# Sixteen gate units as seven half-size products each, beside a running recurrence

## The reference, cut to what matters

```
h     = rmsnorm(x)
proj  = h @ w_in                       # q, k, v | r, k, v of the recurrence | gates (4096 columns)
o_a   = diff_attention(q, k, v)        # 8 heads
o_b   = rwkv7(proj)                    # 32 heads of 64; 4 chunks of 64 tokens; state S per head
gates = sigmoid(proj[gate columns] + b_gate)
mix   = (gates[:2048] * (o_a @ w_branch_a) + gates[2048:] * (o_b @ w_branch_b)) @ w_out
x     = x + rmsnorm(mix);  x = x + rmsnorm(swiglu(rmsnorm(x)));  then the second block
```

## Time and profile before

| | us |
|---|---|
| median of 3 runs (3976.82 to 3977.19) | 3977.06 |
| the profiled execution | 3979.2 |
| its span | 3977.4 |
| TensorE busy | 3846.1 (97%) |
| VectorE busy | 1747.7 (44%) |
| GpSimd busy | 1233.2 (31%) |
| ScalarE busy | 599.5 (15%) |

### The profile page before, as it was taken

The page is one execution under the profiler, slowest core; times in us unless marked ns, Lnnn a source line. Parts: engine busy times, 40 slices in busy tenths (PEclk is TensorE's granted clock), DMA queues, the critical chain, the costliest instruction groups (busy, mean ns, idle before and its releaser), DMA issues.

```text
span 3977.4 us, 65016 instructions
## 1 busy us (share of the span) xinstructions
PE 3846.1 (97%) x28196; PEld 3553.6 (89%) x28196; DVE 1747.7 (44%) x3073; ACT 599.5 (15%) x1314; POOL 1233.2 (31%) x779
## 2 busy tenths in 40 slices
PE   8999999999999998999999999989998899999997
PEld 7888888888878998999999998878797899999997
DVE  1344425550121623111125446552522688888544
ACT  0333311111111111000000000132402211111001
POOL 0000000003320865777760000000250577775000
PEclk9999999999999998999999999999999999999999
DMA  6566654457553443444445454428242344444542
GB/s 229 211 221 219 219 214 159 176 187 225 181 193 139 175 149 117 168 167 168 169 162 170 162 188 183 156 103 227 81 159 85 124 167 168 167 167 159 175 157 78
DMA packets 109117, 668.80 MB, mean 168 GB/s; under 512 B 23056, under 2 KB 27472, under 8 KB 78496
## 3 DMA queue, kind: packets, MB, share of 16 engines
q1 hardware_dynamic: 64208, 549.01, 38.2%
q0 software_dynamic: 21088, 69.73, 6.0%
q10 hardware_dynamic: 23536, 45.92, 3.2%
HBM read 611.34 MB, written 53.25 MB: 167 GB/s over the span
## 4 chain that ended last, share of the span: by engine, by line
PE 92%; DVE 3%; ACT 2%; issue 1%; POOL 1%; POOLq 1%; DVEq 1%; DMA 0%; ACTq 0%
PE product_bank L553 47%; PE product_bank L601 31%; PE product_bank L395 3%; PE mixer_bank L745 1%; PE mixer_bank L761 1%; ACT xT L862 0%; PE mixer_bank L1274 0%; PE mixer_bank L1288 0%; PE mixer_bank L1125 0%; POOL arena L525 0%; POOLq L524 0%; POOL arena L522 0%; POOLq L521 0%; PE product_bank L2237 0%; PE mixer_bank L2199 0%
## 5 line engine op out<-in xcount | busy, mean ns | idle before, releaser
L601 PE MATMUL product_bank<-hT,weight_ring 128*128 128x256 f32 x3712 | 825.0, 380 | 1.6 <-ACT out_stage L640 1.6
L601 PEld LDWEIGHTS product_bank<-hT,weight_ring 128*128 128x128 f32 x3712 | 700.6, 190 | 106.2 <-issue 12.0
L553 PE MATMUL product_bank<-hT,weight_ring 128*128 128x128 f32 x3648 | 453.6, 276 | 11.0 <-DVEq L1631 5.8
L553 PEld LDWEIGHTS product_bank<-hT,weight_ring 128*128 128x128 f32 x3648 | 432.2, 193 | 13.1 <-DVEq L1631 6.0
L553 PE MATMUL product_bank<-arena,weight_ring 128*128 128x128 f32 x3168 | 394.6, 275 | 0.0
L553 PEld LDWEIGHTS product_bank<-arena,weight_ring 128*128 128x128 f32 x3168 | 374.8, 192 | 0.6
L577 DVE TENSOR_TENSOR arena<-product_bank,arena 128x128 f32<-128x128 f32 x126 | 36.7, 291 | 721.1 <-PE product_bank L553 721.1
L520 POOL TENSOR_TENSOR arena<-weight_ring 128x1024 f32<-128x1024 f32 x88 | 211.0, 2398 | 449.7 <-PE product_bank L553 279.6
L2626 DVE SCALAR_TENSOR_TENSOR arena<-arena 128x256 f32<-128x256 f32 x176 | 321.8, 1867 | 14.6 <-ACT arena L2591 11.2
L523 POOL TENSOR_TENSOR weight_ring<-weight_ring 128x1024 f32<-128x1024 f32 x110 | 270.0, 2455 | 0.0
L553 PE MATMUL product_bank<-hT,arena 128*128 128x128 f32 x2016 | 247.4, 277 | 0.1
(11 more groups left out here) (494 smaller groups left out, 5303.5 us busy)
## 6 DMA issues: line engine op xcount, KB each, us to landing
weight_ring<-in_weights SPq DMA_DIRECT2D x213, 2048.0 KB, 8.0
weight_ring<-in_weights SPq DMA_DIRECT2D x128, 512.0 KB, 5.7
weight_ring<-in_weights SPq DMA_DIRECT2D x64, 384.0 KB, 5.7
units<-out_stage ACTq DMA_DIRECT2D x87, 256.0 KB, 7.8
rwkv_keep<-arena ACTq DMA_DIRECT2D x16, 1282.0 KB, 6.3
arena<-rwkv_keep POOLq DMA_DIRECT2D x8, 1280.0 KB, 7.2
arena<-units POOLq DMA_DIRECT2D x36, 256.0 KB, 3.4
arena<-units POOLq DMA_DIRECT2D x48, 128.0 KB, 6.0
```

The source lines that it names most:

```text
L553: mm = pe.matmul(bank[:, at * P:at * P + P], lhs[:, j, :], rhs[:, j, :], start=g == 0 and n in (0, 3) and j == 0, stop=g == n_groups - 1 a ...
L601: mm = pe.matmul(psg[b][:, half * T:half * T + T], lhs, rhs, start=k == 0, stop=k == 15)
```

## The change

Part 1: the gate units are done as sevens, in two groups of four block pairs each, so that a unit is 14 products of 8 records. A unit still has four pieces in TensorE's list, now of 4, 3, 4 and 3 products. The four combinations of the source are made at the start of the kernel into `xT`, which is loaded again from its input during the `out` stage, as are two constants whose space is used.

Part 2: GpSimd makes the weight sums of a group into one buffer per group, so the sum for (unit u, group g) waits until TensorE has used (u - 1, g). The sums of unit 0 stand in the list of the heads, behind the wait for head 5; the others in `rw2_pool`, with the operands' transfers between them.

Part 3: VectorE's list gets the gates' recombinations: the one of unit u stands at quarter 186 + 4u. ScalarE stores the unit's result a unit later.

Part 4: a half's operands come in 8 and 7 transfers instead of 20 and 19; the first group's second half, its last transfer and the storing of the inverse go to SyncE's queue.

```diff
@@ stream_weights
+                if n == UNIT_AT["gates", 6][0]:
+                    store_inverse(sp)
+                if n == UNIT_AT["gates", 8][0]:
+                    rw2_operands(sp, 0, 1)
+                    rw2_rest(sp, 0)
+                if n == UNIT_AT["out", 0][0]:
+                    load_again(sp)
@@
-        SEVENS = ("branch_b", "out", "ffn_in", "ffn_out", "out2", "up2", "down2")
+        SEVENS = ("gates", "branch_b", "out", "ffn_in", "ffn_out", "out2", "up2", "down2")
+        EARLY = ("gates",)
+        GROUPS_OF = {n: GROUPS if n in LONG else 2 if n in EARLY else 1 for n in SEVENS}
@@
+        def early_quarters(pe, name, src, combined, sums):
+            half = lambda blocks, g: [v[:, 4 * g:4 * g + 4, :] for v in blocks]
+            for u in range(PLAN[name].units):
+                steps = unit_sevens(pe, name, u, lambda g: half(source_blocks(src), g), lambda g: sums(u, g),
+                                    lambda g: half(combined, g))
+                for n, _ in enumerate(steps):
+                    if n in (3, 6, 10):
+                        yield
+                yield
@@
+        def rw2_operands(eng, n, half):
+            if n == 0:
+                eng.wait_ge(sem("inverse_stored"), 16)
+                eng.wait_ge(sem("attn_head_done"), DA_HEADS)
+            else:
+                eng.wait_ge(sem("rw2_Y_sum"), NCH * (n - 1) + 2 * half + 2)
...
+            for par in range(2):
+                for head in range(2):
+                    eng.dma_start(r2m[tokens(head, par), :, 2 * head + half, :],
+                                  mu[GT * n:GT * n + GT, par, half, :, head, :].rearrange("g s t -> s g t")).then_inc(got, 16)
@@ rw2_pool
-                    for g in range(GT):
-                        for par in range(2):
-                            for head in range(2):
-                                pool.dma_start(r2m[tokens(head, par), g, 2 * head + half, :],
-                                               mu[GT * n + g, par, half, :, head, :]).then_inc(got, 16)
...
+            for u, g in [(u, g) for u in range(1, 6) for g in range(2)] + [(6, 0)]:
+                sum_gates(pool, u, g)
+            rw2_operands(pool, 0, 0)
+            between = {(9, 1): (1, 0), (11, 0): (1, 1), (12, 0): (1, None), (13, 1): (2, 0), (15, 0): (2, 1), (15, 1): (2, None)}
+            for u, g in [(6, 1)] + [(u, g) for u in range(7, 16) for g in range(2)]:
+                sum_gates(pool, u, g)
+                if (u, g) in between:
+                    n, half = between[u, g]
+                    if half is None:
+                        rw2_rest(pool, n)
+                    else:
+                        rw2_operands(pool, n, half)
@@ da_pool
                 if h >= 2:
                     pool.wait_ge(sem("attn_head_done"), h - 1)
...
+                if h == 7:
+                    sum_gates(pool, 0, 0)
+                    sum_gates(pool, 0, 1)
@@
+        def sum_gates(pool, u, g):
+            if u:
+                group_used(pool, "gates", u - 1, g)
+            sum_weights(pool, "gates", u, g, gates_sums_of(u, g))
@@
+        def gates_product_dve(dve):
+            yield
+            for u in range(16):
+                for _ in range(4):
+                    yield
+                row, o = gates_kept(u)
+                wait(dve, stored[o], 16 * (row // RING))
+                kept_ = ostage[:, o, :]
+                recombine_dve(dve, "gates", u, gates_first[u % 2], *gates_temps, kept_[:, 0:T], kept_[:, T:2 * T])
+                dve.drain().then_inc(sem("gates_kept"), 1)
@@ VectorE's list
-            run(rw1_dve(dve))
-            weave(inv_dve(dve), da_dve(dve), inverse_steps)
-            run(rw2_dve(dve))
+            combine_source_dve(dve, "gates", source_blocks(hT), early_combined)
...
+            elsewhere = (None for _ in range(4 * 45))
+            dense = chain(elsewhere, gates_product_dve(dve))
+            beside(dense, rw1_dve(dve), beside_rw1, RW1_LEAD)
+            beside(dense, heads_and_inverse(), beside_da, DA_LEAD)
+            beside(dense, rw2_dve(dve), beside_rw2, RW2_LEAD)
```

More of the change, by code:

```diff
@@ L452, in group_used @@
         def group_used(eng, name, u, g):
-            pos, half = group_pos(name, u, g)
-            if name in LONG and half == 0:
+            pos = group_pos(name, u, g)[0]
+            if GROUPS_OF.get(name, 1) > 1 and g % 2 == 0:
                 eng.wait_ge(sem("sevens_halves_used"), sevens_half(name, u, g))
@@ L1229, in rw2_pe, with rw2_rest_loaded @@
+        def rw2_loads(half, n):
+            if half and n == 0:
+                return "rw2_first_in1", 16 * 7
+            return f"rw2_in{half}", 16 * (8 - half) * (n + 1 - half)
+        def rw2_rest_loaded(n):
+            return ("rw2_in_all", 16 * n) if n else ("rw2_first_in_all", 16)
         def rw2_pe(pe):
@@ L1373, in group @@
                         last = dve.tensor_tensor(obT[:, b, :], d, kept_all("g", g), ALU.mult)
-                last.then_inc(sem("rw2_group_done"), 1)
-                yield
+                    if pair == GT // 2 - 1:
+                        last.then_inc(sem("rw2_group_done"), 1)
+                    yield
             for n in range(RW_TILES // GT):
@@ L1555, in build, with gates_sums_of, gates_kept, store_gates @@
         bb_out = [arena[:, at:at + 512].rearrange("p (h t) -> p h t", h=2) for at in (12288, 13836)]
+        early_combined = combined_source(xT)
+        flat_y = yT.rearrange("p b t -> p (b t)")
+        gates_sums = {True: [flat_y[:, 2048:3584], (flat_y[:, 3584:4096], flat_y[:, 1024:1536], flat_y[:, 1536:2048])],
+                      False: [flat_y[:, 2048:3584], (flat_y[:, 3584:4096], r2_free, arena[:, 18704:19216])]}
+        gates_first = [const("gram_mask"), const("later")]
+        gates_temps = (const("past_mask")[:, 0:P], const("past_mask")[:, P:384])
+        BESIDE_DA = 6
+        def gates_sums_of(u, g):
+            return gates_sums[u < BESIDE_DA][g]
+        def sum_gates(pool, u, g):
+            if u:
+                group_used(pool, "gates", u - 1, g)
+            sum_weights(pool, "gates", u, g, gates_sums_of(u, g))
+        def gates_kept(u):
+            row = UNIT_AT["gates", u][2]
+            return row, row % RING
+        def store_gates(act, u):
+            row, o = gates_kept(u)
+            act.wait_ge(sem("gates_kept"), u + 1)
+            act.dma_start(units[row, :, :], ostage[:, o, :]).then_inc(stored[o], 16)
+        def gates_product_act(act):
+            for u in range(16):
+                yield
+                yield
+                if u:
+                    store_gates(act, u - 1)
+                yield
+                long_first_act(act, "gates", u, gates_first)
+                yield
+        def gates_product_dve(dve):
+            yield
+            for u in range(16):
+                for _ in range(4):
+                    yield
+                row, o = gates_kept(u)
+                wait(dve, stored[o], 16 * (row // RING))
+                kept_ = ostage[:, o, :]
+                recombine_dve(dve, "gates", u, gates_first[u % 2], *gates_temps, kept_[:, 0:T], kept_[:, T:2 * T])
+                dve.drain().then_inc(sem("gates_kept"), 1)
+        def load_again(sp):
+            sp.dma_start(xT[:, :, :], t_in["xT"]).then_inc(sem("x_again"), 16)
+            a = CONST_AT["later"][0]
+            sp.dma_start(consts[:, a:], t_in["consts"][:, a:]).then_inc(sem("consts_again"), 16)
         def gate_loads(sp):
@@ L2779, in _, with heads_and_inverse @@
             pre_norm_dve(dve, "mix_pre", "g_mix_pre", "mix_in")
-            run(rw1_dve(dve))
-            weave(inv_dve(dve), da_dve(dve), inverse_steps)
-            run(rw2_dve(dve))
+            dve.drain()
+            combine_source_dve(dve, "gates", source_blocks(hT), early_combined)
+            def heads_and_inverse():
+                inverse = inv_dve(dve)
+                for n, _ in enumerate(da_dve(dve)):
+                    for _ in range(inverse_steps(n)):
+                        next(inverse, None)
+                    yield
+                run(inverse)
+            elsewhere = (None for _ in range(4 * 45))
[3 more added lines that the diff above has]
+            beside(dense, rw2_dve(dve), beside_rw2, RW2_LEAD)
+            run(dense)
             gates_dve(dve)
             out_dve(dve)
+            dve.wait_ge(sem("x_again"), 16)
             post_norm_dve(dve, "mix_post", "x_mixed")
```

86 lines of the change are left out of this document (48 added, 38 removed).

## The result

| | before | after |
|---|---|---|
| median of the runs, us | 3977.12 (3976.82 to 3979.01, 4 runs) | 4023.60 (4013.26 to 4032.76, 4 runs) |
| the profiled execution | 3979.2 | 4032.76 |
| its span | 3977.4 | 4030.9 |
| mean granted clock of TensorE | 0.986 | 0.977 |

The ratio is 1.0115 with a 95% interval of 1.0087 to 1.0143: slower, by 46 us, and outside the predicted range. The profiled execution of after is the slowest of its four, so its waits are to be read as those of a time 9 us over the median.

What follows compares the result with a forecast made beforehand. TensorE, busy for 97% of the span, was taken as the bound. -21.0 + 2.6 + 7.4 + 2.8 + 10.2 = +2.0 us took the median from 3977.06 to 3979.1, called "the same" (3971 to 3986); full range 3964 to 3991.

Steps and rivals of the forecast that it cites:

- Lead quarters: Last gate quarters before the recurrence: two sums and GpSimd's operand issuing take 15.3 us against 12.5; stall 2.8 us (2 to 5).
- late operands: Rival at the recurrence's start: operands issued later, in 16.6 us, make TensorE wait 3 to 6 us; 3983 to 3985; chance 0.09.
- The gain: Gate units as sevens: each goes from 13.82 to 12.51 us, 0.89 us per product; sixteen units save 21.0 us.
- GpSimd's sums: Gates' weight sums at half width: 5.0 us each (4.8 to 6.0), fitting the 6.25 us of TensorE's other half unit.
- Start of the gates: Unit 0's first sum, in turns with VectorE's inverse, is ready at 841 where TensorE wants it at 838.36; stall 2.6 us.
- Turn-taking and the heads: Heads 6 and 7: GpSimd's additions and VectorE's two-operand SBUF instructions alternate on the memory; stall 7.4 us (0 to 16.7).
- VectorE as the bound in head 6: Slow rival: six sums hold VectorE back to 55 us against TensorE's 39.9; 15 to 16.7 us stall; 3988.4; chance 0.20.
- A group's end: Recurrence groups 0 and 1: TensorE waits 6.6 us for the second pair, 5.1 more than before; 10.2 us in all.
- The other operand calls: Operand issuing beside the recurrence: priced at nothing, sums being 3 us ahead; without that lead up to 1 us each, five times.
- the bounds above: The terms' stated limits: start 0 to 3 us, heads 0 to 16.7, lead quarters 2 to 5, groups' ends 5.2 or 10.2.
- How the numbers follow: Closing step: chances 0.46 same, 0.25 faster, 0.20 and 0.09 slower; range from 3964 to 3991 us.
- The cover: Fast rival in the heads: half-width additions never make VectorE late; -13.0 us in all, 3964.1; chance 0.25.

Runs made afterwards that it cites:

- experiment 1: The changed kernel with GpSimd's two drains in each of the gates' 32 weight sums replaced by waits on a semaphore its additions raise; 3993.21 us, ratio 1.0045.
- experiment 3: The changed kernel with the first group's first half of operands issued on SyncE's queue instead of by GpSimd; 3994.98 us, ratio 1.0040.
- experiment 11: Experiment 8's kernel with the semaphore in the sums of the gates and `branch_b` alone, later sums keeping their drains; 3959.07 us, ratio 0.9960.
- Experiment 7: Experiment 1's kernel with VectorE centring a group's second pair before the recombination that stood in front of it; 3988.74 us, ratio 1.0043.
- experiment 6: The kernel before with semaphore waits instead of drains in all of GpSimd's weight sums; 3980.08 us against 3978.10, ratio 1.0006.
- experiment 8: The changed kernel with semaphores in all GpSimd sums, operands by SyncE, inverse over after head 4, unit 0's sums earlier, second pair centred first; 3970.16 us, ratio 0.9983.
- experiment 9: The kernel before with the semaphore in place of drains in `branch_b`'s sums alone; 3970.38 us against 3978.37, ratio 0.9983.
- experiment 2: The changed kernel with a drain and one tiny GpSimd addition at the kernel's start; 4014.55 us, ratio 1.0090.
- experiment 4: The changed kernel with the triangular inverse spread over heads 0 to 4 instead of 0 to 6; 4005.23 us, ratio 1.0066.
- experiment 5: The changed kernel with one more GpSimd drain right behind head 6's loads; 4005.69 us, ratio 1.0070.

## Why the prediction was wrong

**The step that failed** is "Lead quarters", and with it the sentence on the sums: "That suffices, by 1.2 us, as long as GpSimd does nothing else and nobody holds it up." The step priced sum (6, 1) behind the operand calls at 5.0 us, the calls at what it takes to issue them, and the stall at 2.8 (2 to 5). The sum took 23.6 us from 948.00 (18.45 of them in its drain) and the stall was 21.8. The prediction counted the transfers' issue on GpSimd's queue but not that the next drain waits for them to land. Experiments 1 and 3 show it in two ways: with no drain the stall is 3.3, and with no transfers ahead of the drain it is none.

The cause could have been read ahead. Before has such a gap in a sum of `branch_b` directly behind six transfers of GpSimd's own, which land in 4.0 to 5.5 us:

```profile
1357.52 2.35 POOL L522 TENSOR_TENSOR arena<-arena,weight_ring 128x1024 f32<-128x1024 f32 x1 [4.38 <-issue]
```

(The last of the six is issued at 1350.2 and so lands at about 1355.7, 1.8 us ahead of this row.) It also has one of the other kind, 6.70 us at 1283, with the last transfer issued 92 us before. TensorE waits 2.8 and 4.5 us behind them. The prediction took its price of a sum from a later one with no transfers near.

This step is not the whole miss. With the drains out of the gates (experiment 1) the time is 3993.21 where 3979.1 was predicted, still over the range's 3991. In that profile `branch_b` starts 19.1 us later than in before: -21.0, +29.4 for the waits, 7.0 of them for the late operands, and +10.5 for TensorE's busy time, 425.4 us instead of 414.9, at a clock of 0.97; together 18.9.

Point by point:

- **The gain** of 21.0 is right where the clock is up: 0.89 us per product. That the clock would be 1.00 throughout was taken from the earlier trace rows and held only as long as TensorE had no waits. This is the second error: 14.1 us of busy time in after, 10.5 in experiment 1, 3.8 in experiment 11, which has few waits left.
- **GpSimd's sums**: 5.0 us priced; alone, one runs from 915.34 to 920.65, 5.31 us.
- **Start of the gates**: 2.6 priced, 9.6 measured. The drain again, here by its count of transfers; with the semaphore it is 2.3.
- **Turn-taking and the heads**: right in kind, and the size in experiment 1 is 6.7 for 7.4. The rows of after at 866 us, with the earlier trace rows's picture at half width:

```profile
865.95 1.80 POOL L534 TENSOR_TENSOR yT<-yT,weight_ring 128x512 f32<-128x512 f32 x1
866.69 1.66 DVE L1179 TENSOR_TENSOR arena<-arena,yT 128x572 f32<-128x572 f32 x1
867.70 1.78 POOL L535 TENSOR_TENSOR weight_ring<-weight_ring 128x512 f32<-128x512 f32 x1
868.43 1.62 DVE L1176 TENSOR_TENSOR yT<-arena 128x530 f32<-128x530 f32 x1
```

Both are stretched, 1.27 to about 1.8 and 0.74 (the 128x572 operation just before these rows) to about 1.65. An addition ends 1.1 us after VectorE's operation, and VectorE's 0.6 us after the addition, so each does its work when the other is through. The Trainium skill ("SBUF — State Buffer", Who interferes with whom) says of two such instructions that the second blocks until the first is over, and these rows agree. The rival built on it, VectorE as the bound in head 6 with 15 to 16.7 us of stalls, isn't seen in any profile.

- **A group's end**: 6.6 priced, 6.7 measured, in groups 0 and 1 alone. Experiment 7 takes the 1.8 us of the recombination out of it. The 2.5 us that were put down to GpSimd's additions weren't tried alone.
- **The other operand calls**, "These I put at nothing". Two of them put 7.0 and 7.6 us into a drain, at 1029 and 1114; behind the others the drain comes later and takes 0.2 to 0.7. TensorE waits only 1.6 and 2.2 us for these sums, because they are made ahead there.
- **The range**: the forecast's 3971 to 3986 are put down to "the bounds above", but these bounds add up to 3963.3 and 3991.0, which is the full range given under "How the numbers follow". Neither holds the result.
- **The rivals**: late operands happened as well, 7.0 us (3 to 6 priced), hidden in after behind the larger stall. The cover did not hold. What decided stood in no rival: a wait of the helper engine for its own transfers.

## What to carry to other kernels

On an engine that both computes and issues transfers, price a drain as a wait for those transfers' landing plus, as the gaps here suggest, 0.08 us for each transfer since the last drain, and give dependent instructions a semaphore of their own or the transfers another queue. A wait for a semaphore isn't always better: a stalled helper also leaves the engine beside it unhindered, and taking its stall away moved the wait to that engine (7.1 us in the NSA heads). Price a stall of TensorE with what follows it: 59 us of idle time in after's stretch came with 14 more of busy time at the lower clock; and when a gain doesn't arrive at the end, compare the start of one late instruction in both traces, and the stretch behind the last instruction as well.

## What the hardware did that had not been expected

- GpSimd's drain waits for transfers that GpSimd has issued: 18.45 us behind transfers with a median landing of 19.6 us, 6.96 and 7.55 behind such with 8.4 and 8.5. The wait on a semaphore of the additions themselves doesn't.
- Behind transfers that have long landed a drain still takes time, and the time goes with their number since the last drain: 0.40 us for 3, 1.55 for 17, 4.90 for 58, 7.68 for 92, some 0.08 us apiece. An early drain at an idle place takes it over. If none comes in the later sums at all, the end of the program is 6.3 to 7.3 us longer, as in experiments 6 and 8.
- What the engine does in that time no row shows, and the count isn't all of it. Four first drains cost less than their count: 1.56 us behind 151 transfers in experiment 1, which is what the last 17 of them cost in after, 1.31 behind 149 in experiment 11, 6.70 behind 256 in before and 7.19 behind 262 in experiment 9. It looks as if something had taken part of the count over by then; what it was is open.
- Transfers of the same `m_units` blocks take 19.6 us to land beside the heads' end when GpSimd issues them, and 9.8 on SyncE's queue in the same kernel at about the same time. Why wasn't tried.
- After a wait of 9.6 us TensorE's first products came every 1.84 and 1.71 us instead of 0.89, some 4 us long; the stretch with the 21.8 us wait has a granted clock of 0.87.
- The runs of some kernels lie far apart: 20 us in after, 26 in experiment 1 and 18 in experiments 7, 8 and 9, against 2 to 7 in before. It doesn't go with the waits: experiments 2, 4 and 5 have nearly all of after's and lie 4 to 6 us apart. That stays open.
